# Embedding gate, mixer, retention and MLP: read-outs, splits and state updates in another order

## What is computed

```python
# first block
h = rms_norm(x, g_mix);  z = h @ w_in
a = mla(...)                       # four attention heads
r = hgrn2(...)                     # four gated linear recurrences, in chunks, forward and backward
x = x + concat([a, r]) @ w_o
h = rms_norm(x, g_ffn)
x = x + (silu(h @ w_gate) * (h @ w_up)) @ w_down
gate = sigmoid(rms_norm(x, g_ple) @ w_ple_gate)      # the embedding gate
x = x + gate * (p @ w_ple_proj)
# second block
h = rmsnorm(x, g_pre_mix_2);  proj = h @ w_in_2
y_ret = retention(q, k, v, g)      # four heads, chunks, forward and backward states, layer norm
y_sgu = spatial_gate(u, sv)
x = x + rmsnorm((sigmoid(a_ret) * y_ret + sigmoid(a_sgu) * y_sgu) @ w_out, g_post_mix)
h2 = rmsnorm(x, g_pre_ffn)
x = x + rmsnorm(conv_gated_mlp(h2, w_up, conv_w, conv_b, w_down), g_post_ffn)
```

## Time and profile before

| what | value |
|---|---|
| median of three runs | 1670.34 us |
| the profiled execution | 1669.57 us |
| its span, first to last instruction | 1668.2 us |
| TensorE busy | 1625.5 us (97%) |
| VectorE busy | 876.2 us (53%) |
| ScalarE busy | 654.7 us (39%) |
| mean granted share of TensorE's clock | 0.993 |

### The profile page before, as it was taken

How to read it: one execution, slowest core, us unless ns; L and a number is a source line. 1 busy time by engine, 2 the same in 40 slices (tenths; PEclk the granted TensorE clock), 3 DMA queues, 4 the chain that set the end, 5 groups by cost and what they waited for, 6 DMA issues and landing times.

```text
span 1668.2 us, 18650 instructions
## 1 busy us (share of the span) xinstructions
PE 1625.5 (97%) x7857; PEld 1342.1 (80%) x7857; DVE 876.2 (53%) x1164; ACT 654.7 (39%) x799; POOL 11.7 (1%) x25
## 2 busy tenths in 40 slices
PE   7999999999999999997999999999998999999998
PEld 6777777788888888886798898888886878888887
DVE  6546646574444532256755644455444777766313
ACT  4445757443222321153443433224334444444312
POOL 1000000000000000000000000000000000000000
PEclk9999999999999999999999999999998999999999
DMA  5321010113323322222221232323323223322332
GB/s 163 95 75 52 26 51 26 68 59 126 100 91 101 101 101 86 92 95 101 76 83 55 73 98 85 102 76 101 101 76 101 76 76 101 101 90 88 114 101 76
DMA packets 120274, 144.28 MB, mean 86 GB/s; under 512 B 6009, under 2 KB 109776, under 8 KB 120192
## 3 DMA queue, kind: packets, MB, share of 16 engines
q1 hardware_dynamic: 118768, 139.87, 25.4%
q0 software_dynamic: 1232, 3.16, 0.6%
q10 hardware_dynamic: 192, 0.07, 0.0%
HBM read 140.99 MB, written 2.10 MB: 86 GB/s over the span
## 4 chain that ended last, share of the span: by engine, by line
PE 91%; DVE 4%; ACT 3%; issue 1%; DMA 0%; SPq 0%; DVEq 0%; ACTq 0%
PE bank L373 27%; PE bank L375 27%; PE bank L374 27%; PE bank L885 1%; PE bank L647 1%; PE bank L646 1%; PE bank L665 1%; PE bank L713 1%; DVE slab_lo L1039 1%; ACT slab_hi L1782 1%; PE bank L868 1%; PE bank L694 1%; PE bank L422 1%; PE bank L591 1%; PE bank L708 1%
## 5 line engine op out<-in xcount | busy, mean ns | idle before, releaser
L373 PE MATMUL bank<-h_hi,slab_hi 128*128 128x512 f32 x1192 | 473.4, 397 | 14.7 <-DVE h_lo L1044 5.9
L1039 DVE TENSOR_TENSOR slab_lo<-slab_raw,slab_hi 128x2048 fp32r<-128x2048 f32 x130 | 296.0, 2278 | 337.5 <-ACT slab_hi L1782 337.2
L375 PE MATMUL bank<-h_hi,slab_lo 128*128 128x512 f32 x1192 | 466.8, 392 | 0.0
L374 PE MATMUL bank<-h_lo,slab_hi 128*128 128x512 f32 x1192 | 466.6, 391 | 0.0
L1782 ACT ACTIVATE slab_hi<-slab_raw 128x2048 fp32r<-128x2048 f32 x130 | 246.4, 1896 | 169.6 <-DMA slab_raw<-in_w_down 142.8
L373 PEld LDWEIGHTS bank<-h_hi,slab_hi 128*128 128x128 f32 x1192 | 225.5, 189 | 68.7 <-issue 14.5
L374 PEld LDWEIGHTS bank<-h_lo,slab_hi 128*128 128x128 f32 x1192 | 225.6, 189 | 47.5 <-issue 1.4
L375 PEld LDWEIGHTS bank<-h_hi,slab_lo 128*128 128x128 f32 x1192 | 225.3, 189 | 47.7
L1081 DVE TENSOR_TENSOR tmp<-bank,x_rstd_rows 128x512 f32<-128x512 f32 x98 | 66.7, 687 | 99.4 <-PE bank L375 99.2
L373 PE MATMUL bank<-slab_hi,h_hi 128*128 128x256 f32 x320 | 91.8, 287 | 0.0
L375 PE MATMUL bank<-slab_hi,h_lo 128*128 128x256 f32 x320 | 90.5, 283 | 0.0
(11 more groups left out here) (406 smaller groups left out, 2170.6 us busy)
## 6 DMA issues: line engine op xcount, KB each, us to landing
slab_raw<-in_w_in SPq DMA_DIRECT2D x40, 1024.0 KB, 4.9
slab_raw<-in_w_up SPq DMA_DIRECT2D x33, 1024.0 KB, 5.1
slab_raw<-in_w_down SPq DMA_DIRECT2D x22, 1024.0 KB, 4.9
slab_raw<-in_w_gate SPq DMA_DIRECT2D x11, 1024.0 KB, 5.1
slab_raw<-in_w_o SPq DMA_DIRECT2D x4, 1024.0 KB, 5.0
slab_raw<-in_w_ple_gate SPq DMA_DIRECT2D x4, 1024.0 KB, 4.9
slab_raw<-in_w_ret_o SPq DMA_DIRECT2D x4, 1024.0 KB, 5.0
slab_raw<-in_w_sgu_o SPq DMA_DIRECT2D x4, 1024.0 KB, 5.1
```

Source lines behind the costliest of these rows:

```text
L373: T.matmul(ps, a_hi, b_hi, start=start, stop=False, skip_group_check=skip)
L374: T.matmul(ps, a_hi, b_lo, start=False, stop=False, skip_group_check=skip)
L375: return T.matmul(ps, a_lo, b_hi, start=False, stop=stop, skip_group_check=skip)
L1039: V.tensor_tensor(w_lo[j][:, 0:n], raw[j][:, 0:n], w_hi[j][:, 0:n].bitcast(F32), ALU.subtract).then_inc(slab_lo, 1)
```

## The change

Four edits. In the embedding gate both engines' loops are replaced by an order written out by hand: the read-outs of tiles 0 to 3 first, the splits of PLE+4, IN2 and IN2+1 at other places among the work on the tiles, and the tiles' later work in between. In the first mixer `head_scaled` stands ahead of the split, and `state_updates` in steps 6 and 7 stands right behind the split instead of behind the additions. In the retention the second half slab of steps 1 and 2 goes to bank 4 instead of bank 0, and `ret_state_updates` stands ahead of `ret_means`. In the MLP the split of slab UP2+5 is done in step 3 instead of step 4, on VectorE and ScalarE.

```diff
 # TensorE, retention
-                b = (7, 4 if s in (0, RET_SLABS - 1) else 0)[t]
+                b = (7, 4 if s in (0, 1, 2, RET_SLABS - 1) else 0)[t]
 # VectorE, first mixer
-            split(MIX + n + 1)
             if n >= 3 and n % 2:
                 head_scaled(n // 2 - 1)
+            split(MIX + n + 1)
+            if n >= 6:
+                state_updates(n)
             if n >= 5:
                 head_gated(n - 5)
...
-            state_updates(n)
+            if n < 6:
+                state_updates(n)
 # VectorE, embedding gate
-        for n in range(4):
-            if n:
-                split(PLE + 3 + n)
-                for k in range(2 * n - 2, 2 * n):
-                    norm_tile(3, k, "g_pre_mix_2")
-                sum_tiles(x2_k, squared, 2 * KT, 2 * n - 2, 2 * n)
-            for t in range(2):
-                f = 2 * n + t
-                gt = tmp[f % 4]
-                if f >= 4:
-                    V.wait_ge(x_done, f - 3)
-                scaled(("pg", f), gt)
-                V.wait_ge(ple_sigmoid, f + 1)
-                V.wait_ge(vector_step, step(V.tensor_tensor(gt, gt, proj[:, f, :], ALU.mult)))
-                V.tensor_tensor(xT[:, f, :], xT[:, f, :], gt, ALU.add).then_inc(x_done, 1)
+        def gate_scaled(f):
+            if f >= 4:
+                V.wait_ge(x_done, f - 3)
+            scaled(("pg", f), tmp[f % 4])
+        def gate_added(f):
+            gt = tmp[f % 4]
+            V.wait_ge(ple_sigmoid, f + 1)
+            V.wait_ge(vector_step, step(V.tensor_tensor(gt, gt, proj[:, f, :], ALU.mult)))
+            V.tensor_tensor(xT[:, f, :], xT[:, f, :], gt, ALU.add).then_inc(x_done, 1)
+        for f in range(4):
+            gate_scaled(f)
+        gate_added(0)
+        gate_added(1)
+        split(PLE + 4)
+        gate_added(2)
+        gate_added(3)
+        norm_tile(3, 0, "g_pre_mix_2")
+        gate_scaled(4)
+        split(IN2)
+        norm_tile(3, 1, "g_pre_mix_2")
+        gate_added(4)
+        for k in range(2, 4):
+            norm_tile(3, k, "g_pre_mix_2")
+        gate_scaled(5)
+        sum_tiles(x2_k, squared, 2 * KT, 0, 2)
+        gate_added(5)
+        norm_tile(3, 4, "g_pre_mix_2")
+        sum_tiles(x2_k, squared, 2 * KT, 2, 4)
+        norm_tile(3, 5, "g_pre_mix_2")
+        gate_scaled(6)
+        gate_added(6)
+        gate_scaled(7)
+        split(IN2 + 1)
+        gate_added(7)
...
-        sum_tiles(x2_k, squared, 2 * KT, KT - 2, KT, squares_summed)
+        sum_tiles(x2_k, squared, 2 * KT, 4, KT, squares_summed)
 # VectorE, retention
+            if 1 <= s <= HEADS:
+                ret_state_updates(s - 1)
             if 2 <= s < HEADS + 2:
                 ret_means(s - 2)
-            if 1 <= s <= HEADS:
-                ret_state_updates(s - 1)
 # VectorE, MLP (ScalarE the same)
-                if 2 * n + s2 == 2:
-                    split(UP2 + 4)
-                if 2 * n + s2 == 3:
-                    V.wait_ge(conv_right, 2 * n + 2)
-                if 2 * n + s2 > 3:
+                if 2 * n + s2 in (2, 3):
+                    split(UP2 + 2 * n + s2 + 2)
+                if 2 * n + s2 == 4:
+                    V.wait_ge(conv_right, 2 * n)
+                if 2 * n + s2 > 4:
                     split(UP2 + 2 * n + s2 + 1)
 # ScalarE, embedding gate
-        for n in range(4):
-            if n:
-                split(PLE + 3 + n)
-            for t in range(2):
-                f = 2 * n + t
-                emptied(("pg", f))
-                A.activation(tmp[f % 4], tmp[f % 4], ACT.Sigmoid).then_inc(ple_sigmoid, 1)
-                A.wait_ge(x_done, f + 1)
-                A.activation(h_hi[:, f, :], xT[:, f, :], ACT.Identity, ...)
-                A.activation(x2[:, f, :], xT[:, f, :], ACT.Square).then_inc(squared, 1)
+        for f in range(4):
+            gate_sigmoid(f)
+        split(PLE + 4)
+        gated_features(0)
+        gated_features(1)
+        split(IN2)
+        gate_sigmoid(4)
+        gated_features(2)
+        gated_features(3)
+        gate_sigmoid(5)
+        gated_features(4)
+        gated_features(5)
+        gate_sigmoid(6)
+        split(IN2 + 1)
+        gate_sigmoid(7)
+        gated_features(6)
+        gated_features(7)
```

## The result

The changed kernel takes 1648.01 us, the median of 4 runs (1647.64 to 1650.32), against 1670.3 us before: a ratio of 0.9876, 95% interval 0.9864 to 0.9888 (the quotient of the two medians is 0.9867, inside the interval). A second set of 4 runs gave 1646.9 us (1646.02 to 1647.46), ratio 0.9867 [0.9853, 0.9882]; the seven runs of the kernel before beside it have a median of 1667.77, 20.9 us more. The profiled execution took 1650.32 us, its span 1649.0; it was the slowest of its four.

The account below looks back on a forecast made before the run. TensorE was taken as the bound, busy 1625.5 of 1668.2 us, so only its idle time and half clock could be won. 13.3 + 4.4 + 1.3 + 1.4 = 20.4 us off 1670.34 gave 1649.9 us, range 1644 to 1658.

Parts of the forecast that it names:

- The gate: Embedding gate: reading banks first removes TensorE's waits, late starts and one half-clock stretch, a gain of 13.3 us.
- the cover: Embedding gate: VectorE's chain ends 1.3 us ahead of TensorE's want of the sum of squares.
- the first rival: Embedding gate: the chain stays too long, eight sigmoids costing 0.85 us each; 1656.3 us, chance 0.11.
- the count by positions: Embedding gate: the gain counted as the squares' start, 800.91 less 787.4, giving 13.5 us.
- The mixer: First mixer: earlier state updates and the scaled head ahead of the split together gain 4.4 us.
- the scaled head: First mixer, steps 3, 5 and 7: scaling the head ahead of the split frees a bank sooner, gaining 0.4 us.
- the states' term: First mixer, step 6: earlier state updates remove 2.3 us of wait with late start and 1.7 of half clock, 4.0.
- The retention: Retention: bank 4 ends two waits of 0.49 us, 0.65 each with late start, gaining 1.3 us.
- The MLP: Convolution MLP: the split stall moves one slab on; one half-clock stretch behind it leaves 1.4 us gain, two leave nothing.
- The untouched norm: Norm ahead of the MLP, not edited: half clock there may shift by one stretch, 1.7 us either way.
- The slower rival: MLP: the vector chain sets the pace; at 2.6 us over per slab pair, 1675.9 us, chance 0.03.
- the second rival: MLP: the stall goes away altogether, 3.65 + 1.7 us better; 1644.6 us, chance 0.10.

Follow-up runs that it names:

- e7_margin: Changed kernel with five useless VectorE instructions in a row behind the gate's fifth split: 1650.55 us, ratio 0.9886.
- e11_scaled_behind: Changed kernel with the first mixer's scaled head behind the split again: 1647.77 us in one run.
- e10_means_first: Changed kernel with the retention's means ahead of the state updates again, bank 4 kept: 1648.99 us in one run.
- retention alone: Kernel before with only the retention's edit: 1666.85 us, ratio 0.9987.
- mixer alone: Kernel before with only the first mixer's edit: 1664.48 us, ratio 0.9971.
- gate alone: Kernel before with only the embedding gate's edit: 1654.7 us, ratio 0.9914.
- e8: Changed kernel with 6, 5 and 13 useless matmuls in the three waits of the norm ahead of the MLP: 1645.61 us, ratio 0.9863.
- e4_mlp: Kernel before with only the convolution MLP's edit: 1667.46 us, ratio 0.9989.
- e9_both: Changed kernel with every later MLP split one step sooner and useless matmuls in the waits of the norm ahead: 1640.41 us, ratio 0.9826.
- e5_all_sooner: Changed kernel with every later split of the MLP also one step sooner: 1643.71 us, ratio 0.9848.

## Why the prediction was right, point by point

The forecast of 1649.9 us lies 1.9 above the first median and 3.0 above the second; both, and all runs, are in the range.

**The gate** (13.3, measured 13.7). The mechanism is the one described: the read-outs come first, and slabs and features are ahead of TensorE. The first two slabs' end stands at 749.27 (753.3 less the 4.03 by which the gate begins sooner), so the squares start 34.02 us behind it; the step said 34.1. The chain is 782.46 - 749.27 = 33.2 us, where the step counted 32.8. The term that was mis-sized is the cover, 0.83 for 1.3, and e7_margin shows that it is real. The sigmoids' 0.8 us came out as 0.87, so the first rival (eight times 0.85) is refuted. The 13.3 was the mean of two counts; the count by positions, 13.5, was the nearer. Both took the half clock here, one stretch of 3.4 us, from one execution. The mixer's, the retention's and the MLP's kernel, whose gate is as before, have two such stretches in their traces, and in two of them one stands behind the wait of 2.26 us, behind which the profiled execution of before had none. Against such executions the gate's edit is worth up to 1.7 us more.

**The mixer** (4.4, measured 4.39). The states were to be ready at 304.6 and are at 304.8, and the stretch at half clock is gone, as 4.0 said. That leaves 0.4 for the scaled head, but e11_scaled_behind gives it 0.15. So the states' term measured 4.24 for 4.0 and the head's 0.15 for 0.4: the sum was right by two misses that cancel, and by luck of another kind: 1.7 of the 4.0 is the half clock behind the wait of 2.17 us, which was one stretch of 3.4 us in the profiled execution, 6.8 us in those of the gate's and the retention's kernel, and none in that of the MLP's.

**The retention** (1.3, measured 1.54). Both waits are gone and none came. For the second head the updates end at 869.6, and the half slab is wanted at about 871.3, a margin of 1.7 for the forecast 1.5. Without the new order it is gone, which e10_means_first shows.

**The MLP** (1.4, measured 0.31). The stall moved to where the step put it: 1342.98 with 18.91 added is 1361.89, and 1361.9 was the number. It is 3.26 us long for 3.5. What was mis-sized is what follows. The step took one stretch of half clock of 3.4 us; the profiled execution had 6.8 by the window above (before: the earlier trace rows), and "two leave nothing" is what it measured. In other executions of the same stall there was less, or none:

| execution | wait, us | half clock behind it, us |
| --- | --- | --- |
| before, retention alone, mixer alone | 3.56 | 6.8 |
| gate alone | 3.56 | 3.4 |
| changed, first | 3.26 | 6.8 |
| e7, e10, e11 | 3.22 to 3.26 | 3.4 |
| changed again, e8, MLP alone | 3.22 to 3.25 | none |

So one stretch lies in the middle of what happens, and the profile of any one execution doesn't decide the term; by the ratio of e4_mlp it is 1.8, with an interval from a gain of 4.5 to a loss of 0.7. The Trainium skill (TensorE: Matmul & The Clock Gate, section The HAM clock gate) says that the number of slow matmuls varies from run to run of one kernel; the table agrees, for a stall in mid-kernel. The rule that the prediction drew from the same section, that a moved stall brings a slow stretch along, holds in most of these executions and not in all: 3 of 7 with the moved stall had none.

The half clock also accounts for the 1.9 us between forecast and median, as far as the record goes. The forecast started from one execution of before and inherited its half clock. The profiled execution of after took 1650.32, 0.4 above the forecast, with half clock in 17 us; the other three took 2.1 to 2.7 less, at mean granted clocks of 0.995 to 0.997 for its 0.994, and the changed kernel run again spent 6.8 us at half clock by its trace. For executions without a profile the record has the mean granted clock, but not where it fell. Of the 21 runs of before, nine took 1666.29 to 1667.52 us, all at 0.994, and twelve took 1669.94 to 1672.75, at 0.990 to 0.992. The forecast was added to a median of the second group, 1670.34. From the 1667.8 of the later set it would have been 1647.4, beside the 1646.9 measured there: the sum of 20.4 was nearer to the mark than the time it gave.

**The untouched norm**: -0.35, within the ± 1.7 it was given. **The slower rival**, that the vector chain sets the MLP's pace, is refuted twice: after the moved wait TensorE has none over 0.2 us, and in e9_both, with every split sooner, VectorE is busy 39.01 of 50 us and TensorE all 50. That the stall could go away altogether, the second rival, was wrong for the reason given against it, and right for a longer change: 1643.71 us with all splits sooner.

## What to carry to other kernels

A stall at a just-in-time step can move by one step when one producer is moved by one step; here it went only when all that follow were moved too. When a chain of small instructions is taken off the critical path, count how far ahead it ends (here 0.83 us of 33) and treat that as the budget for anything added to it. And where a kernel has a few waits of 1 to 4 us, count the half clock behind them as a spread, not a number: compare executions, and their mean granted clocks, before explaining 2 us.

## What the runs showed that I had not expected

**The same wait, another clock.** 3.25 us of waiting were followed by 6.8 us at the lower level, by 3.4 or by none, behind the same instruction. The kernel before spreads over 6.5 us (1666.29 to 1672.75 in 21 runs), in two groups that differ in mean granted clock, 0.994 and 0.990 to 0.992; e9_both, at 1.000 in all four runs, spreads over 0.7. And in two of 13 traces the clock also fell where TensorE had not waited at all.

**A slow TensorE at a full granted clock.** One execution of e5_all_sooner took 5410.36 us, the other three 1643.45 to 1643.71. Window from 10 to 510 us of that execution, then of the changed kernel run again:

```profile
10.00:510.00 500.00, 499.98 (x749) 304.35 (x750) 92.37 (x139) 76.08 (x100) 1.63 (x3) 1.00 0.08 24
```

```profile
10.00:510.00 500.00, 496.55 (x2474) 395.73 (x2475) 289.55 (x433) 246.29 (x320) 2.39 (x4) 1.00 0.24 76
```

TensorE did 749 matmuls where it does 2474, at a granted clock of 1.00, while a split on VectorE took 2.28 us as ever. The profile shows no cause, and it happened once in the runs of this study; the comparison leaves that execution out.
